# Sums of the modulation projections taken by VectorE's 32x32 turns in place of TensorE's transposes

## The reference, cut to what matters

```python
c = silu(condition)                   # two of them: for x and for the context, each 2048 long
mod = c @ w_mod + b_mod               # w_mod: 2048 x 12288; six kinds of 2048 columns
sh1, sc1, gt1, sh2, sc2, gt2 = split(mod, 6)
h = modulate(rmsnorm(h), sh1, sc1)    # h * (1 + scale) + shift; x and context both
h = h + gt1 * mix(h)
h = h + gt2 * swiglu(modulate(rmsnorm(h), sh2, sc2))
```

## Time and profile before

| | |
|---|---|
| times of three runs | 2287.92, 2291.16, 2290.82 us |
| median | 2290.82 us |
| span of the profiled execution | 2285.8 us |
| TensorE busy | 2266.4 us, 99% |
| VectorE busy | 1556.3 us, 68% |
| ScalarE busy | 1109.7 us, 49% |
| mean granted TensorE clock | 0.997 of full speed |

### The profile page before, as it was taken

One profiled execution on the slowest core, in us unless ns is written; L12 is line 12 of the kernel. 1 busy time (PEld: TensorE's weight loads), 2 busy tenths in 40 slices (PEclk: granted clock), 3 DMA queues, 4 the chain that ended last, 5 costly groups with the idle time before them and its releaser, 6 DMA issues.

```text
span 2285.8 us, 28964 instructions
## 1 busy us (share of the span) xinstructions
PE 2266.4 (99%) x10345; PEld 1864.5 (82%) x10345; DVE 1556.3 (68%) x1869; ACT 1109.7 (49%) x1531; POOL 223.5 (10%) x361
## 2 busy tenths in 40 slices
PE   9999999999999999999999999999999999999998
PEld 7888888888888888888878877787888888888886
DVE  7886778778867877887767664556555545555556
ACT  6446455555545545545463463545444344444444
POOL 0121001111111111110011000000210011100110
PEclk9999999999999999999999999999999999999999
DMA  8983679978888888886677664564665666656663
GB/s 311 331 272 97 206 235 320 317 267 293 275 281 287 273 301 269 272 280 215 220 242 245 209 203 129 186 220 158 210 203 194 207 207 198 207 185 201 195 195 126
DMA packets 250005, 528.12 MB, mean 231 GB/s; under 512 B 22144, under 2 KB 22544, under 8 KB 248592
## 3 DMA queue, kind: packets, MB, share of 16 engines
q1 hardware_dynamic: 214256, 405.32, 54.2%
q0 software_dynamic: 33664, 116.17, 14.8%
q10 hardware_dynamic: 1952, 4.85, 0.6%
HBM read 517.87 MB, written 4.21 MB: 228 GB/s over the span
## 4 chain that ended last, share of the span: by engine, by line
PE 97%; DVE 1%; ACT 1%; DMA 0%; issue 0%; SPq 0%; ACTq 0%; DVEq 0%; POOLq 0%
PE acc L1798 30%; PE acc L1807 29%; PE acc L1802 29%; PE tp L1869 2%; PE m L1880 1%; PE acc L1820 0%; PE acc L1825 0%; PE acc L1830 0%; PE tp L2206 0%; PE tp L2224 0%; PE tp L2218 0%; PE acc L2000 0%; PE tp L2131 0%; PE acc L1853 0%; PE acc L1851 0%
## 5 line engine op out<-in xcount | busy, mean ns | idle before, releaser
L1090 DVE TENSOR_TENSOR wlo<-wring,whi 128x1024 fp32r<-128x1024 f32 x762 | 919.5, 1216 | 562.6 <-ACT whi L565 455.4
L565 ACT ACTIVATE whi<-wring 128x1024 fp32r<-128x1024 f32 (+1 forms) x510 | 532.1, 1047 | 720.4 <-PE acc L1807 719.3
L1798 PE MATMUL acc<-whi,xhi 128*128 128x512 f32 x2056 | 558.5, 393 | 0.1
L1802 PE MATMUL acc<-whi,xlo 128*128 128x512 f32 x2056 | 550.0, 389 | 0.0
L1807 PE MATMUL acc<-wlo,xhi 128*128 128x512 f32 x2056 | 549.9, 389 | 0.0
L1802 PEld LDWEIGHTS acc<-whi,xlo 128*128 128x128 f32 x2056 | 386.0, 188 | 81.1
L1807 PEld LDWEIGHTS acc<-wlo,xhi 128*128 128x128 f32 x2056 | 386.0, 188 | 80.7
L1798 PEld LDWEIGHTS acc<-whi,xhi 128*128 128x128 f32 x2056 | 381.2, 188 | 86.3 <-issue 9.0
L575 ACT ACTIVATE whi<-wring 128x1024 fp32r<-128x1024 f32 x266 | 280.8, 1059 | 319.8 <-PE acc L1807 318.1
L1120 DVE SCALAR_TENSOR_TENSOR macc<-mring,csil,macc 128x512 f32<-128x512 f32 x480 | 344.0, 747 | 29.3 <-DMA mring<-w_mod 23.0
L460 POOL DMA_DIRECT2D mring<-w_mod x192 | 138.9, 724 | 1047.4 <-DVE macc L1120 998.9
(11 more groups left out here) (277 smaller groups left out, 1313.7 us busy)
## 6 DMA issues: line engine op xcount, KB each, us to landing
wring<-w_up SPq DMA_DIRECT2D x216, 512.0 KB, 4.7
wring<-w_down SPq DMA_DIRECT2D x216, 512.0 KB, 5.1
mring<-w_mod POOLq DMA_DIRECT2D x192, 512.0 KB, 5.3
wring<-w_in SPq DMA_DIRECT2D x184, 512.0 KB, 5.2
wring<-w_gate SPq DMA_DIRECT2D x88, 512.0 KB, 4.3
wring<-w_out SPq DMA_DIRECT2D x64, 512.0 KB, 4.9
tmpT<-blk POOLq DMA_DIRECT2D x128, 32.0 KB, 3.4
gbig<-ctx_in POOLq DMA_DIRECT2D x2, 1024.0 KB, 8.1
```

The source lines that it names most:

```text
L565: act.activation(whi[:, piece_slot(c, piece), 0:half], wring[:, g4, piece * half:(piece + 1) * half], ACT.Copy).then_inc(hi_done, 1)
L1090: dve.tensor_tensor(wlo[:, h4, 0:half], wring[:, g4, piece * half:(piece + 1) * half], whi[:, h4, 0:half].bitcast(F32), ALU.subtract).then ...
L1798: pe.matmul(acc[:, 2 * pair + t, :], hi[:, tile, t * P:(t + 1) * P], whi[:, h4, w], start=(tile == starts), stop=False)
L1802: pe.matmul(acc[:, 2 * pair + t, :], lo[:, tile, t * P:(t + 1) * P], whi[:, h4, w], start=False, stop=False)
```

## The change

The sums over partitions are made by VectorE alone. `turn_mod` turns `macc` by 32x32 blocks into `tmpT`: column block b of 32 columns and partition quarter a of 32 partitions become a block in which the free axis runs over the 32 old partitions. `sum_mod` adds these up along the free axis (128 x 512 to 128 x 16), copies three partition quarters beside the first, adds the four, and copies three of the four columns of each result back to the partition quarters 1 to 3. Last it adds the bias into `modT`. Each of these five steps waits by a semaphore for the one before it, all on VectorE. The order of the modulation work around it moves by one or two slots. TensorE's and ScalarE's part is gone, and so are the waits of ScalarE's squares and of TensorE's `scores` step that guarded the banks `m0` and `m1`.

```diff
-        modsum = sb("modsum", [P, 2, KG])
+        parts = vrows[:, 0, :].rearrange("p (w a b) -> p w a b", w=2, a=4)
+        sums = vrows[:, 1, 0:2 * 4 * KG].rearrange("p (w k q) -> p w k q", w=2, k=KG)
+        LAST_SPREAD = (2, 2, 1, 1, 1, 1, 0, 0)
         MLP_MODS = {**{g: (SC2, 2 if g == 3 else 1) for g in range(0, 7)},
-                    **{g: (SC1, 1) for g in range(7, 15)},
-                    **{g: (GT1, 2 if g == 18 else 1) for g in range(15, 22)},
-                    **{g: (SH2, 1) for g in range(22, 30)}}
-        MLP_REDUCED = {7: SC2, 15: SC1, 22: GT1, 30: SH2}
-        SH1_STEPS = {**{6 + s: s for s in range(8)}, **{15 + s: s for s in range(8)}, **{24 + s: s for s in range(6)}}
-        SH1_TURNED, SH1_SUMMED, SH1_TAKEN, SH1_SET = (13, 22), (15, 24), (15, 24), (16, 25)
+                    **{g: (SC1, 1) for g in range(8, 16)},
+                    **{g: (GT1, 2 if g == 21 else 1) for g in range(16, 23)},
+                    **{g: (SH2, 1) for g in range(23, 31)}}
+        MLP_TURNED = {7: SC2, 16: SC1, 23: GT1, 31: SH2}
+        MLP_SUMMED = {7: SC2, 18: SC1, 24: GT1, 31: SH2}
+        SH1_STEPS = {**{6 + s: s for s in range(8)}, **{16 + s: s for s in range(8)}, **{26 + s: s for s in range(6)}}
+        SH1_TURNED, SH1_SUMMED = (14, 24), (15, 25)
...
@@ on ScalarE, with its calls @@
-            def sum_mod(dual):
-                for who in range(2 if dual else 1):
-                    bank = m0 if who else m1
...
-                    for j in range(KG):
-                        cols = slice(j * P, (j + 1) * P)
-                        act.activation(bank[:, cols], bank[:, cols], ACT.Copy,
-                                       accum_out=modsum[:, who, j:j + 1]).then_inc(mod_summed, 1)
...
+            def turn_mod(dual):
+                dve.wait_ge(mod_acc, c.at("ma", 8))
+                for who in (1, 0) if dual else (0,):
+                    last = dve.transpose(tmpT[:, 1 - who, :], macc[:, who, :])
+                last.then_inc(mod_turned, 1)
+                c.add("turns")
+
+            def sum_mod(kind, i, dual):
+                n = 2 if dual else 1
+                nth = c.at("sets", 1)
+                dve.wait_ge(mod_turned, nth)
+                for who in range(n):
+                    last = dve.reduce_sum(parts[:, who, 0, :], tmpT[:, 1 - who, :].rearrange("p (b j) -> p b j", j=32), AX_X)
+                last.then_inc(mod_summed, 1)
+                dve.wait_ge(mod_summed, nth)
+                for a in range(1, 4):
+                    last = dve.tensor_copy(parts[0:32, 0:n, a, :], parts[32 * a:32 * a + 32, 0:n, 0, :])
+                last.then_inc(mod_gathered, 1)
+                dve.wait_ge(mod_gathered, nth)
+                for who in range(n):
+                    last = dve.reduce_sum(sums[0:32, who, :, :].rearrange("p k q -> p (k q)"),
+                                          parts[0:32, who, :, :].rearrange("p a b -> p b a"), AX_X)
+                last.then_inc(mod_reduced, 1)
+                dve.wait_ge(mod_reduced, nth)
+                for q in range(1, 4):
+                    last = dve.tensor_copy(sums[32 * q:32 * q + 32, 0:n, :, 0], sums[0:32, 0:n, :, q])
+                last.then_inc(mod_spread, 1)
+                dve.wait_ge(mod_spread, nth)
+                for who in range(n):
+                    dve.tensor_tensor(modT[:, who, bass.ds(i * 4 + kind * KT, 4)], sums[:, who, :, 0],
                                      vecs[:, 1, bass.ds(i * 4 + kind * KT, 4)], ALU.add).then_inc(mod_set, 1)
...
@@ mlp_chunk on VectorE @@
+                    elif first and g == 4:
+                        sum_mod(SH1, 3, True)
+                    if g in MLP_TURNED:
+                        if last and g > min(CTX_TURNS):
+                            dve.wait_ge(tp_free, c.at("q", 2))
+                        turn_mod(MLP_TURNED[g] == SC1)
+                    if g in MLP_SUMMED and not (last and g == 31):
+                        sum_mod(kind, i, kind == SC1)
...
@@ on TensorE, with their calls @@
-            def reduce_mod(per_nb, dual):
-            def reduce_gate(per_nb):
...
-                        pe.wait_ge(mod_set, 32)
```

More of the change, by code:

```diff
@@ L841, in round_group @@
                 def round_group(g):
[L842 to L845, removed]
+                    round_groups(1)
                     if last and g in CTX_TURNS:
@@ L866, in _ @@
             root_and_scale(2, u_g, u_g)
-            with c.loop(act, MLP_CHUNKS - 1, 1, g=32, q=8, half=4, blk=4, ha=4, ssq=4 * T, mt=5):
+            with c.loop(act, MLP_CHUNKS - 1, 1, g=32, q=8, half=4, blk=4, ha=4, ssq=4 * T):
                 mlp_chunk()
@@ L1123, in mod_steps @@
                     c.add("m")
[L1125 to L1135, removed]
-                                      vecs[:, 1, bass.ds(i * 4 + kind * KT, 4)], ALU.add).then_inc(mod_set, 1)
@@ L1364, in _ @@
                 if n == 0:
[L1365 to L1366 removed]
+                    sum_mod(SH1, 2, True)
                 elif n < 3:
@@ L1369, in _ @@
             remain_added(3)
-            take_mod(True)
-            set_mod(SH1, 3, True)
+            turn_mod(True)
             c.add("ssq", T * KG)
@@ L1419, in _ @@
             norm_scale(2, u_g, u_g)
-            with c.loop(dve, MLP_CHUNKS - 1, 1, g=32, q=8, hi=8, m=32, ma=80, mt=5, msum=5 * KG) as i:
+            with c.loop(dve, MLP_CHUNKS - 1, 1, g=32, q=8, hi=8, m=32, ma=80, sets=4, turns=4) as i:
                 mlp_chunk(i)
@@ L1571, in in_blocks @@
                             k = 4 * part + kg
-                            mod_steps(SPREAD[k], sum(SPREAD[0:k]), False)
-                            if k == 7:
-                                set_gate(GT2, which)
+                            spread = LAST_SPREAD if which == 3 else SPREAD
+                            mod_steps(spread[k], sum(spread[0:k]), False)
+                            if sum(spread[0:k]) == MSTEPS and sum(spread[0:k - 1]) < MSTEPS:
+                                turn_mod(False)
+                                sum_mod(GT2, which, False)
             in_blocks(C_IN, 0)
@@ L1871, in turn_rows @@
                     c.add("q")
-            def reduce_mod(per_nb, dual):
-                c.add("ma", per_nb)
-                pe.wait_ge(mod_acc, c.at("ma", 8))
-                for who in range(2 if dual else 1):
-                    bank = m0 if who else m1
-                    for j in range(4):
-                        last = pe.transpose(bank[:, j * P:(j + 1) * P], macc[:, who, j * P:(j + 1) * P], ident)
-                    last.then_inc(mod_turned, 1)
-            def reduce_gate(per_nb):
-                c.add("ma", per_nb)
-                pe.wait_ge(mod_acc, c.at("ma", 8))
-                for j in range(4):
-                    last = pe.matmul(m1[:, j:j + 1], macc[:, 0, j * P:(j + 1) * P], ones, start=True, stop=True)
-                last.then_inc(mod_reduced, 1)
             pe.sem_inc(piece_multiplied, HSLOTS)
@@ L2081, in mlp_chunk @@
                             turn_rows(blk, 2)
-                        if 4 * j + kg in MLP_REDUCED and not (last and 4 * j + kg == 30):
-                            reduce_kind(MLP_REDUCED[4 * j + kg])
                         turn_ctx(4 * j + kg)
@@ L2095, in _ @@
             mlp_chunk(True)
-            with c.loop(pe, MLP_CHUNKS - 1, 1, g=32, q=8, ma=80, ha=4, half=4, blk=4):
+            with c.loop(pe, MLP_CHUNKS - 1, 1, g=32, q=8, ha=4, half=4, blk=4):
                 mlp_chunk()
@@ L2244, in in_blocks @@
                         pe.wait_ge(h_added, H_MLP - 1 + n)
-                    which, part = MOD_PAIRS[p].get(name, (None, 0))
                     for kg in range(2 if name == "l" else 4):
```

61 lines of the change are left out of this document (16 added, 45 removed).

## The result

The changed kernel takes 2293.7 us (median of 20 runs, 2290.45 to 2295.71), the kernel before 2289.61 us (20 runs, 2287.42 to 2292.22). The ratio is 1.0016, 95% interval [1.0009, 1.0022]: 0.16% slower, within the 0.2% that the prediction calls no change. Forecast were 2274.8 us. The profiled execution of the changed kernel took 2292.85 us, with a span of 2291.1 us.

What follows compares the result with a forecast made beforehand. TensorE, busy 99% of the span, was taken to bound the kernel. Span 2285.8 less 17.0 of removed work plus 1.0 of stall gave 2269.8; plus 5.0 to the median, 2274.8 us, range 2270 to 2284.

Steps and rivals of the forecast that it cites:

- 2285.8 - 17.0 + 1.0 = 2269.8 us of span: Whole kernel: profiled span less the work TensorE loses, plus one allowed stall.
- at 0.91 us everywhere in the chunks: Expected sign in the profile after: in the MLP chunks, L1807 is followed by L1798 at 0.91 us.
- four rivals: VectorE's small operations cost 0.69 us; VectorE becomes the bound; something else sets the pace; VectorE can't do it (no own chance).
- TensorE's 17.0 us: Reductions leaving TensorE's path: 7.1 us for 8 dual, 5.5 for 12 x alone, 3.4 for 4 GT2, 1.0 for a wait.
- the 5.0 us added from span to median: Whole kernel: the profiled span lies 5.0 us under the median of 2290.8, so 5.0 was added to the forecast span.
- ScalarE at nothing: Dropping ScalarE's 112 activations of 255 ns was costed at nothing, as ScalarE idles 51% of the span and waits for TensorE.
- VectorE's costs: New turns and sums: 0.69 us per turn or long reduction, 0.19 per small operation; VectorE rises from 1556 to about 1634 us.
- the first two rivals: Small VectorE operations cost 0.69 us each, about 2290 (0.09 with the third rival); VectorE becomes the bound, about 2347 (0.06).
- All of it hidden: VectorE's turns and sums fit the 3.1 us free per slot and VectorE's lead, so TensorE waits at most 1.0 us, once.
- The stall of 1.0 us: TensorE waiting once for VectorE's remainder in slots 22 to 24 of the last MLP chunk, where the lead comes out near zero.
- the debt: VectorE work beyond a slot's free time, taken from its lead: in all 5.8 us in slots 22 to 24, last chunk.
- a lower clock: Listed sign that would make the prediction wrong: a lower granted clock behind a wait of L1807; no size given.

Runs made afterwards that it cites:

- e2_before_shifted: The kernel before with an unused 32-byte tile per partition behind modsum, so later tiles lie 32 bytes higher: 2306.23 us, ratio 1.0080 to the kernel before.
- e1_same_addresses: The changed kernel with an unused 32-byte tile per partition where modsum stood, giving later tiles their addresses of before: 2273.85 us, ratio 0.9930 to the kernel before.
- e8_more_reductions: e7_defer_sh2 with one more long VectorE reduction, result unused, at each of the 16 sums for one row alone: 2273.69 us, ratio 0.9926 to the kernel before.
- e3_two_pads: The changed kernel with 64 unused bytes per partition where modsum stood: 2290.94 us, ratio 1.0009 to the kernel before.
- e10_w_and_x_shifted: The changed kernel with 32 unused bytes ahead of whi alone; whi, wlo, xhi, xlo begin at 32 mod 64, ahi, alo, bhi, blo at 0: 2292.76 us.
- e9_all_shifted: The changed kernel with 32 unused bytes ahead of whi and 32 where modsum stood, so all operand tiles begin at 32 mod 64: 2274.03 us.
- e5_xhi_shifted: The changed kernel with 32 unused bytes ahead of xhi and xlo; these begin at 32 mod 64, ahi, alo, bhi, blo at 0: 2311.5 us.
- e4_ahi_only: The changed kernel with 32 unused bytes ahead of the phases holding ahi and alo; these begin at 0 mod 64, bhi and blo at 32: 2280.19 us.
- e7_defer_sh2: e1_same_addresses with the last two SH2 steps, their turn and sum moved from the last MLP chunk to the pass behind it: 2272.31 us.

## Why the prediction was wrong

**The step that failed** is the sum, "2285.8 - 17.0 + 1.0 = 2269.8 us of span". It lets every matmul that the diff doesn't name keep its 0.91 us for four, and the text says so for the profile after ("at 0.91 us everywhere in the chunks"). The first line of the diff takes away a tile of 32 bytes, and no term of the sum stands for what moves with it. The runs put there +17.5 us (e2_before_shifted, alone in the kernel before) and 18.0 us (changed kernel against e1_same_addresses, record by record), which is the whole gain. None of the four rivals was it: they place the loss on VectorE or on another engine that sets the pace, and this one needed no wait at all.

**TensorE's 17.0 us leave its path: right.** With the addresses of before (e1_same_addresses) the span is 2272.1. 2285.8 - 17.0 + 2.2 of wait + 1.5 at the lower clock is 2272.5. The measured median, 2273.85, lies 1 us under the forecast 2274.8. That it is so near is partly luck: the stall was 2.7 us larger than the 1.0 allowed, and the 5.0 us added from span to median was too much: by 20 runs the median of the kernel before is 3.8 us above that span, and that of e1_same_addresses 1.8 us above its own.

**ScalarE at nothing: right.** Its busy time fell from 1109.7 to 1078.1 us, 31.6, and the time of e1_same_addresses needs no gain from that. TensorE's longest wait for it is 1.6 us in the changed kernel.

**VectorE's costs: right.** Forecast were 0.69 for turn and reduction, measured 696 and 680 ns; for the small ones 0.19, measured 0.18 to 0.19 from start to start in the copies. Too low was only the reduction of 64 elements, 251 ns. VectorE came to 1625 us; forecast about 1634. With that the first two rivals fall. The Trainium skill (VectorE: DVE Perf Modes, section "Two Vector instructions with no wait between them"), weighed in the prediction, agrees with the trace: the copies, whose quarters change, start 0.18 us apart at 164 to 171 ns each, without overlap. What the Trainium skill says in the same page's section "Why tensor_reduce can't reduce along partition axis" holds for the one instruction and not for the engine: turn, sum and copies do it in about 4.7 us for a dual one (1.30 + 3.4). That a copy from one quarter to another is no dearer than one within it, as the Trainium skill (Vector Engine (DVE) Microarchitecture Reference, "Bank-to-quadrant routing") says for at most 32 partitions, fits the 164 ns of the copies beside the 162 of the last add (L1139), which stays in its partitions; a copy within one quarter isn't in the trace.

**All of it hidden: right but for one place.** e8_more_reductions adds 16 reductions of 0.68 us there at no cost that is clear of noise. The list of waits has one new entry of TensorE for VectorE.

**The stall of 1.0 us: wrong in place and too small.** Forecast was L1807 waiting for a remainder in slots 22 to 24 of the last chunk. No such wait came: in that chunk the step that waits for its `w_mod` is the second of slot 21, and it waits 1.3 us (at 989.83) where the prediction put up to 2.9. The stall came at the end of that chunk, for the last context bank: 2.2 us, plus 1.5 for the lower clock behind it. The prediction followed the debt from slot to slot only up to 24. The change moves every step of SH2 one slot later, so that the last one stands in slot 30 rather than 29, beside the context's last banks. That the waiting would bring a lower clock stands in the prediction as a thing that would make it wrong, with no price.

**What isn't settled.** The sum of the profiled execution is 2285.8 - 17.0 + 18.1 + 2.2 + 1.5 = 2290.6, measured 2291.1, so little is left over. By medians, the changed kernel is 0.86% above e1_same_addresses, 19.7 us, and e3_two_pads and e10_w_and_x_shifted stand 18 and 19.5 above their aligned partners; what these have beyond 18.1 may be the lower clock, whose stretches differ from one execution to another, but most runs behind the medians have no trace. Which stage in the chip makes 6 ns out of the remainders wasn't tried. Nor were other remainders than 0 and 32 by 64, nor, as said, operands 64 or 128 bytes apart. What decides whether the lower clock follows a wait is open too.

## What to carry to other kernels

A diff that adds, drops or resizes a tile moves all tiles declared behind it: look first for groups of untouched instructions whose mean has changed, and run the change once more with a pad that restores the addresses before you judge its idea. Where TensorE is the bound, give the two operands of its float32r products the same remainder by 64 bytes, and by 256 where that is free, since all fast pairs here had that too. When steps are moved later in a hand-written order, follow the debt to the end of the stage, where the last of them meets what the next stage waits for.

## What the runs showed of the hardware that was not expected

A float32r product of 128x128 by 128x512 takes 6.3 ns more from start to start (0.933 us for four instead of 0.906, 2.8%) if one operand begins at 32 and the other at 0 modulo 64 bytes of its partition, whichever of the two it is. Where both begin at 0 or both at 32 there is no cost (e9_all_shifted). It adds up to 17.5 us in 2880 products (e2_before_shifted), and in the 6336 of e5_xhi_shifted to 37.7 beside a wait of 2.2 us that went. Whether 64 is the modulus, or 128 or 256, these runs can't tell. The Trainium skill (SBUF — State Buffer, section "Operand start alignment") asks only for a multiple of the element's size and says of its own runs that they timed nothing; all the addresses here keep that rule.

The wait of TensorE in front of C_IN was followed by matmuls at nearly half the speed, with a granted clock of 0.94 from 1030 to 1060 us, in four profiled executions: e9_all_shifted (1.9 us of wait), the changed kernel and e1_same_addresses (2.2) and e4_ahi_only (3.2). It was not, with a clock of 1.00, in e3_two_pads (2.1) and e10_w_and_x_shifted (2.5), nor in e7_defer_sh2 (1.2) and e8_more_reductions (1.5). The length of the wait alone doesn't decide it.
